# TensorE matmuls of constants in eight places of the mixers, and group norm sums over 32 columns

## The reference

```python
# layer 0: mixer0 and mlstm
hm, _, _ = mlstm_bidirectional(qm, km, vm, gates_x, st_f, st_b, True)
y_a = window_attention(apply_rope(qa, cos, sin) * attn_scale, apply_rope(ka, cos, sin), va, ka_c, va_c, attn_sink[l])
x = x + g_a * (jnp.concatenate([y_m, y_a], axis=-1) @ w_out[l])
# layer 1: mixer1, retention (ret) and state-space (ssd)
scores = jnp.einsum('bhnid,bhnjd->bhnij', qc, kc) * decay
mu = jnp.mean(yr, axis=-1, keepdims=True)
var = jnp.mean(jnp.square(yr - mu), axis=-1, keepdims=True)
yr = ((yr - mu) * lax.rsqrt(var + EPS)).reshape(b, l, RET_WIDTH) * gn_w
ys = rms_norm(ys.reshape(b, l, SSD_INNER) * jax.nn.silu(z), ssd_norm_w)
# layer 2: mixer2 (MLA)
p = jax.nn.softmax(jnp.einsum('bqhd,bkhd->bhqk', q, k) * ((QK_NOPE + QK_ROPE) ** -0.5), axis=-1)
```

## Time and profile before

| | before |
|---|---|
| median of 3 runs | 1501.13 us (1498.7 to 1503.14) |
| the profiled execution | 1499.47 us, span 1497.6 us |
| granted TensorE clock, mean | 0.971 |
| PE busy | 1418.1 us (95%), 8800 matmul records |
| weight loads (PEld) | 1212.4 us (81%) |
| DVE, ACT, POOL busy | 812.0 (54%), 666.3 (44%), 825.7 (55%) us |
| chain that ended last | PE 51%, DVE 3%, ACT 1% (it is followed back to about 641 us) |

### The profile page before, as it was taken

One profiled execution on the slowest core, in us unless ns is written; L12 is line 12 of the kernel. 1 busy time (PEld: TensorE's weight loads), 2 busy tenths in 40 slices (PEclk: granted clock), 3 DMA queues, 4 the chain that ended last, 5 costly groups with the idle time before them and its releaser, 6 DMA issues.

```text
span 1497.6 us, 22626 instructions
## 1 busy us (share of the span) xinstructions
PE 1418.1 (95%) x8800; PEld 1212.4 (81%) x8800; DVE 812.0 (54%) x1554; ACT 666.3 (44%) x1100; POOL 825.7 (55%) x665
## 2 busy tenths in 40 slices
PE   5989999999999999887999999999999999999997
PEld 3868788999988887544878888888878865999997
DVE  3687667777576687567675333321126657332211
ACT  3445655544543133674442322232226376544442
POOL 0533507999864443554435454544446630699995
PEclk9999999999999999888999999999999999999999
DMA  9656605777775652100445555543333320365664
GB/s 367 258 184 232 256 5 195 261 253 253 239 262 186 203 175 85 42 29 1 150 146 197 197 186 195 186 140 90 104 104 101 114 96 1 113 195 186 184 185 125
DMA packets 71322, 242.59 MB, mean 162 GB/s; under 512 B 7472, under 2 KB 13104, under 8 KB 70832
## 3 DMA queue, kind: packets, MB, share of 16 engines
q1 hardware_dynamic: 68800, 237.15, 47.0%
q10 hardware_dynamic: 2416, 4.00, 0.9%
HBM read 239.02 MB, written 1.05 MB: 160 GB/s over the span
## 4 chain that ended last, share of the span: by engine, by line
PE 51%; DVE 3%; ACT 1%; issue 1%; POOL 0%; DMA 0%; DVEq 0%; ACTq 0%
PE bank L547 15%; PE bank L549 14%; PE bank L548 14%; PE cond_a L968 1%; PE bank L968 1%; PE bank L684 1%; PE bank L685 1%; PE bank L976 1%; PE cond_a L1028 1%; PE bank L688 1%; PE bank L988 1%; PE cond_b L988 1%; PE cond_b L976 0%; ACT w_hi L1286 0%; DVE scratch L2585 0%
## 5 line engine op out<-in xcount | busy, mean ns | idle before, releaser
L1794 POOL TENSOR_TENSOR w_lo<-raw,w_hi 128x512 fp32r<-128x512 f32 (+1 forms) x612 | 773.1, 1291 | 630.6 <-ACT w_hi L1286 619.7
L1286 ACT ACTIVATE w_hi<-raw 128x1024 fp32r<-128x1024 f32 (+3 forms) x301 | 308.9, 1029 | 592.5 <-PE bank L549 511.9
L547 PE MATMUL bank<-h_hi,w_hi 128*128 128x256 f32 (+2 forms) x1604 | 524.7, 327 | 5.9 <-DVE h_lo L1856 2.6
L549 PE MATMUL bank<-h_hi,w_lo 128*128 128x256 f32 (+2 forms) x1604 | 521.4, 325 | 0.0
L548 PE MATMUL bank<-h_lo,w_hi 128*128 128x256 f32 (+2 forms) x1604 | 521.3, 325 | 0.0
L547 PEld LDWEIGHTS bank<-h_hi,w_hi 128*128 128x128 f32 (+1 forms) x1604 | 301.9, 188 | 38.0 <-DVE h_lo L1856 5.8
L549 PEld LDWEIGHTS bank<-h_hi,w_lo 128*128 128x128 f32 (+1 forms) x1604 | 301.9, 188 | 26.4
L548 PEld LDWEIGHTS bank<-h_lo,w_hi 128*128 128x128 f32 (+1 forms) x1604 | 302.1, 188 | 26.0
L547 PE MATMUL bank<-hidden_hi,w_hi 128*128 128x256 f32 (+1 forms) x528 | 167.0, 316 | 0.2 <-POOL w_lo L1794 0.2
L548 PE MATMUL bank<-hidden_lo,w_hi 128*128 128x256 f32 (+1 forms) x528 | 166.9, 316 | 0.0
L549 PE MATMUL bank<-hidden_hi,w_lo 128*128 128x256 f32 (+1 forms) x528 | 166.9, 316 | 0.0
(11 more groups left out here) (416 smaller groups left out, 1771.7 us busy)
## 6 DMA issues: line engine op xcount, KB each, us to landing
raw<-in_up SPq DMA_DIRECT2D x132, 512.0 KB, 3.6
ada_w<-in_ada SPq DMA_DIRECT2D x128, 512.0 KB, 4.5
raw<-in_down SPq DMA_DIRECT2D x48, 448.0 KB, 3.4
raw<-in_out SPq DMA_DIRECT2D x24, 512.0 KB, 3.7
raw<-in_down SPq DMA_DIRECT2D x24, 512.0 KB, 3.6
raw<-in_in SPq DMA_DIRECT2D x24, 512.0 KB, 3.6
arena<-in_ada SPq DMA_DIRECT2D x16, 512.0 KB, 11.8
raw<-in_uq SPq DMA_DIRECT2D x12, 384.0 KB, 3.0
```

Of the source, the lines that this page charges most:

```text
L547: pe.matmul(out, w_h, x_h, start=first, stop=False)
L549: return pe.matmul(out, w_l, x_h, start=False, stop=last)
L1286: act.activation(part_slot(w_hi, f, u), raw_slot(f, u), ACT.Copy).then_inc(s["rounded"], 1)
L1794: pool.tensor_tensor(part_slot(w_lo, f, u)[:, a:b], raw_slot(f, u)[:, a:b], part_slot(w_hi, f, u)[:, a:b].bitcast(F32), ALU.subtract).then ...
```

## The change

A new function `idle(out, *columns)` issues, for each number given, one f32 matmul of `ident` with the first columns of `fixed` into a PSUM bank that is free at that place. Nothing reads the result. It is called in eight places, all on TensorE:

```diff
+            def idle(out, *columns):
+                for n in columns:
+                    pe.matmul(out[:, 0:n], ident, fixed[:, 0:n], start=True, stop=True)
...
@@ mixer0, in the loop over slots, behind chunk(c), and before the last values
+                    if j == 0:
+                        idle(bank[4], 3 * P, 3 * P, 3 * P)
                     turn(2 * j)
...
+                idle(bank[2], 3 * P, P)
                 values(AH // 2 - 1)
@@ mixer1
+                pe.wait_ge(s["sd_tt"], TT)
+                idle(bank[6], *(6 * (3 * P,)))
                 pe.wait_ge(s["rope_ready"], 2)
                 pe.wait_ge(s["taken"], ph["out1"].first_taken)
-                pe.wait_ge(s["sd_tt"], TT)
                 ret_scores(0)
...
                     else:
+                        pe.wait_ge(s["rt_y"], 2)
+                        idle(bank[7], 3 * P, 3 * P, 2 * P)
                         pe.wait_ge(s["rt_p"], 12)
                         spread(0)
...
-                        n = 2 * (TT * i + t)
-                        last = pe.matmul(bank[5][:, n:n + 2], sq_r[i][:, t * P:(t + 1) * P], C1("half_mean")[:, ::64],
+                        n = 32 * (TT * i + t)
+                        last = pe.matmul(bank[5][:, n:n + 32], sq_r[i][:, t * P:(t + 1) * P], C1("half_mean")[:, ::4],
...
                 spread(5)
+                idle(bank[6], 3 * P, 3 * P)
                 pe.wait_ge(s["gn_inv"], 1)
...
                 spread(13)
+                idle(bank[6], 3 * P, 3 * P, P)
                 ssd_weighted(1)
                 spread(14)
                 spread(15)
+                pe.wait_ge(s["sd_y"], 1)
+                idle(bank[5], *(6 * (3 * P,)))
                 ssd_weighted(2)
@@ ScalarE
-            act.activation(gn_inv, bank[5][:, 0:32], ACT.Sqrt, bias=EPS).then_inc(s["gn_std"], 1)
+            act.activation(gn_inv, bank[5][:, ::16], ACT.Sqrt, bias=EPS).then_inc(s["gn_std"], 1)
```

## The result

The changed kernel takes 1506.89 us in the median of 8 runs (1503.93 to 1511.54), the kernel before, in the runs beside it, 1501.81 (1495.31 to 1505.47). The ratio is 1.0035 with a 95% interval of 1.0018 to 1.0052: slower by 0.35%, some 5 us. In a second set of runs on another occasion it was 1.0048 (1.0031 to 1.0064). The forecast was 1505.0, or +0.26%.

The account below looks back on a forecast made before the run. TensorE, busy 95% of the span, was taken as the bound through its work, waits and half-clock stretches. Terms +1.9 +2.6 +0.9 -0.9 -0.4 -0.2 = +3.9 us on the median 1501.13 gave 1505.0 us, range 1496.0 to 1509.5.

Parts of the forecast that it names:

- rival 2: Slower: mixer1's start fillers cost their full 3.9 us, other delays more; +6.8 us, 1507.9 us; chance 0.37.
- The price of a filler: f32 identity matmul on TensorE: 0.645 us for 384 columns, 0.86 for 512; 15.9 us in all eight places.
- A: Three fillers before mixer0's first transposes, where TensorE had no wait: 1.9 us lost (0 if weights set that stage).
- D: Six fillers at mixer1's start, ahead of the big wait, which moves with them: 2.6 us lost (2.1 to 3.9).
- H: Fillers before the second state-space product, delaying VectorE's gate by 1.5 us: 0.9 us lost (0 to 1.5).
- I: Fillers before the third state-space product, 3.87 us against a 2.47 us wait: 0 (0 to 0.5 lost).
- E: Fillers in the 2.46 us wait before the last head pair's decay rows: 0.4 us gained (0 to 1.3).
- F: Group norm sums over 32 columns instead of 2: no cost; 0.2 us gained together with G.
- G: Fillers in the 2.04 us wait before the group spreads: free at 2.4 GHz; 0.2 us gained together with F.
- C: Two fillers in the 1.63 us wait before mixer2's first transposes: 0.9 us gained (0 to 1.7).
- B: Filler in the 1.25 us wait before mixer0's last values, already followed by the high clock: 0.
- Rival 1: Fillers hold 2.4 GHz through both halves of mixer1 and through mixer2: -4.9 us, 1496.2 us; chance 0.18.

Follow-up runs that it names:

- changed_again: The changed kernel run once more, nothing altered; ratio to the kernel before 1.0048, median 1508.75 us.
- no_mixer2: The changed kernel without the two fillers ahead of mixer2's first transposes; ratio to the kernel before 1.0033, median 1506.59 us.
- no_mixer0: The changed kernel without the three fillers ahead of mixer0's first transposes; ratio to the kernel before 0.9989, median 1502.3 us.
- start_moved: The changed kernel with mixer1's six start fillers removed and four put into the wait before the second retention scores; ratio to the kernel before 1.0007, median 1504.26 us.
- only_waits: The kernel before with 32-column group norm sums and fillers only inside mixer waits, including the one before the last state-space product; ratio 0.9969, median 1497.19 us.
- sums_alone: The kernel before with group norm sums over 32 columns and no fillers; ratio to the kernel before 0.9992, median 1500.92 us.
- mixer2_alone: The kernel before with 32-column group norm sums and only the two fillers ahead of mixer2's first transposes; ratio 0.9990, median 1501.09 us.

## Why the prediction was right, and where its steps were not

The sign and the size came out as forecast, 1506.9 for 1505.0, though the median lies nearer to rival 2's 1507.9, and the second set of runs (1.0048, 7 us) beside it. That the sum held is in part luck: three of its terms were off and cancelled. The steps:

- **The price of a filler** held: 1.93 us for three of 384 columns, 3.97 for six, 54 records in all.
- **A, mixer0:** charged 1.9 us, measured 1.9 between profiles of the same clock. Its reading (no idle time ahead, all engines move together, the later waits don't swallow it) was right. The runs say more than 1.9 us, which isn't explained.
- **D, start of mixer1:** charged 2.6 us within 2.1 to 3.9, measured 3.3 in the first profile and 3.9 on average. The mechanism was right: the wait moved and stayed at 4.22 us. The term was under-sized at one step. I let the first value product follow at 627 to 628 us because the low-clock scores "were not ready for VectorE anyway"; less the 2.5 us that the execution was late already, it came at 628.15. The second scores came 3.6 us later and stayed partly at the low clock, so what came back was 0.4 us of wait and 0.3 of clock, not 1.3 us. That is the first profile; in changed_again the low clock covered all of the second scores and reached the product, which came 4.0 us later than before. Rival 2's 3.9 was the better price here. With eighteen fillers the wait was the same to 0.01 us.
- **H:** charged 0.9, measured together with I 0.3 between single profiles and nothing between the averages of seven and four. The product was 1.5 us late as stated, and the delay did not reach the end of the mixer. The end of the range that I gave less weight was the right one.
- **I:** charged 0, measured together with H. The wait and the slow product behind it stayed, as said.
- **E, F, G:** 0.6 us gained in the forecast, as a guess on other executions. mixer1 of the changed kernel takes 94.4 to 95.9 us in its two profiles, 94.4 and 94.5 in no_mixer2 and no_mixer0, and 90.6 to 92.2 in the three without fillers there, on average 94.8 and 91.7. That is 3.1 us: 4.0 more up to the first value product (D), 1.1 less at the last head pair (E), 0.2 more in the rest. E was mis-sized, 0.4 with 1.3 as its most, where a slow product costs 1.7 us and came in three of four profiles without the fillers. The profile that the forecast was read from was the one without it. F alone is nothing, as said, and nothing singles out G; its fillers ran at the low clock in the first profile (2.93 us for the two, where the wait had been 2.04), and the stretch around them was no longer than where they ran fast (25.1 us in start_moved too).
- **C, mixer2:** 0.9 us gained in the forecast; this step is not borne out as a property of the kernel. The first profile seemed to prove more (1.00 for 0.60, attention 1.1 us shorter), but the part ahead was 1.4 us longer, a profile without the fillers was as fast, one with them as slow as before, and the runs show nothing. The sum of both parts averages 572.0 us in nine profiles with them and 572.2 in three without. The failure was to take one execution's low stretch for a property of the place, and half of its price for the worth of a filler.
- **B:** 0, and so it is: mixer0 takes 93.77 us with it (only_waits) and without it (sums_alone).

With the measured terms the sum is +1.9 (A) + 3.1 (mixer1) - 0.3 (C) = +4.7 us for +3.9, against some 5 to 7 us in the two sets of runs. The forecast had 2.9 for mixer1: against the averages D was 1.4 too small, H 0.7 too large, and the gains of E, F and G 0.5 too small. These errors nearly cancelled, and C, worth 0.3 and not 0.9, brought the total up by 0.6.

Rival 1 (the clock held, 1496.2) had its mechanism right where its conditions were met: only_waits fills the waits of 4.22 and 4.85 us and gains 0.31%, 4.6 us, some 2 of them from the last product, which it priced at 2.6, 0.4 to 1.2 from the second retention scores, which it priced at 1.3, and none that can be told from mixer2. The Trainium skill's rule ("TensorE: Matmul & The Clock Gate", section "Why this matters for your kernels") is that an idle gap between bursts of matmuls, if it is long enough, puts the clock back to half. For the long waits the rows agree: left empty, the one before the second retention scores (4.22 to 4.60 us) and the one before the last product (4.00 to 4.85 us) were each followed by slow work in all eleven profiles, and filled in none. Short waits, which the page's row does not cover, went both ways here: the same one of 1.63 us was followed by a low stretch before and by none in no_mixer2. What the rule leaves open is the larger part of the answer here: whether the fast work behind the gap is what anyone waits for.

## What to carry to other kernels

Work that keeps a clock up is free only inside an existing wait, and must stand behind the last thing that others need: ahead of it, it moves the wait and costs nearly its full length (3.6 us of 3.9 up to the second scores at mixer1's start, with the wait left at 4.2 us). It pays where TensorE's own work is the chain behind the wait (some 2 us at the last product, 1.7 at the last head pair), and little where TensorE then stands idle for another engine (3 us behind five norms where 10 to 15 were expected). And one profile can't tell which waits cost the clock: compare stretches over several executions, also those ahead of the place, before a low stretch is priced or a gain believed.

## What the runs showed of the hardware

- Low stretches come and go between executions at the same place: at 112 to 119 us in mixer0 in 6 of 14 profiles, costing 1.65 us each, whether fillers were there or not. In the kernels without fillers at the norms, a double stretch at the norm ahead of mixer2 went with none in the attention, a single one with a low clock there in all but one profile.
- Waits of 4.0 to 4.9 us left empty were followed by slow work each time: the second retention scores (all 16 records) take 4.3 to 5.5 us for 2.85, and the last product 5.04 to 5.39 for 2.80, in 11 of 11 profiles each.
- 11.86 us of uninterrupted f32 matmuls didn't keep the clock through a wait of 4.22 us behind them (second scores 2.90 us, as without them).
- Fillers can themselves run at the low clock, and each then takes twice as long: in mixer2 1.92 us in changed_again for 1.03 in mixer2_alone, and, partly slow, 4.28 us in start_moved for 2.85 in only_waits (at 618.60).
- The last 226 us ran up to 4 us longer in 5 of 14 profiles. In the two compared closely, the same 1285 records started 1.1% further apart, evenly and without idle time, at a granted clock of 1.00. No run tells why.
